# Four slots instead of five in each of the two rings of gathered expert rows

## The chip, the cores and the metric

The kernel runs on one core of one Trainium2 chip. The metric is the device time of one execution in microseconds (us), as the median of several runs. TensorE (PE), VectorE (DVE), ScalarE (ACT) and GpSimd (POOL) each have an instruction stream of their own; SyncE (SP) only issues DMAs here.

## The reference

One decoder layer over 1,024 positions of width 1,024, in float32. Its first half is attention: `h = x + W_out(concat[headnorm(A(xn)), subln(B(xn))])`, where A is a dilated sliding-window attention of 8 heads and B a differential attention of 4 heads with two softmax maps each. The second half is a retrieval over 16,384 single-neuron experts:

```python
def peer_layer(x, w_q, sub_keys, u_table, v_table):
    ...                     # scores of 8 heads against 2 x 128 sub-keys, top 16 of each, top 16 of the 256 sums
    u = u_table[ic]         # per token 128 rows of 1024 floats
    act = gelu(einsum('cd,chkd->chk', xc, u)) * gates
    v = v_table[ic]         # per token another 128 rows of 1024 floats
    return einsum('chk,chkd->cd', act, v)
```

The result is `h + peer_layer(RMSNorm(h))`. Every token picks its own 128 experts, so its u rows and v rows have to be gathered by index.

## The kernel before

The 1,024 tokens are 8 tiles of 128, one token to a partition. A first phase projects all tiles to q, k and v with the whole of w_in in SBUF. Then come stages e = 0 to 9. In stage e the *front* works on tile e: attention maps, output projection, norm, queries, and the selection of the 128 experts of each token. At the same time the *experts* of tile e-1 are worked off. A stage is written out by hand as 64 slots. Slot s of a stage holds two picks, 2s and 2s+1, of the 128 of the tile, and on every engine pieces of the front stand between them: in slots 0 to 19 the attention (lines 501, 517 and 530 on PE, line 839 on DVE, lines 695 and 704 on ACT), in slots 21 to 24 the output projection (line 545), in slots 27 to 50 the expert queries (line 566, whose weights SP loads through a ring of its own), in slots 32 to 55 the selection, and in slots 56 to 59 six operations of DVE of 2,048 elements each (lines 941, 945 and 949). Stage 0 has a front alone; from stage 1 on rows are gathered; stages 8 and 9 have no front.

For pick g, counted over all tiles:

- POOL issues the gather of the u row (`gather_u`, line 408): one row of 1,024 floats, 4 KB, for each of the 128 tokens, 512 KB in all, into slot g % RU of `u_ring`. Before it may issue, DVE must have finished with the row that stood in that slot (`u_used`).
- DVE multiplies that row with the normed token and sums it (`dot_row`, line 1026); the sum goes through Gelu on ACT in groups of 16, and times the gate it is the activation.
- POOL issues the gather of the v row (`gather_v`, line 417), again 512 KB, into slot g % RV of `v_ring`. It has to wait for PE's last use of that slot (`v_used`).
- ACT makes a diagonal matrix of the activations (`make_diag`, line 680), and PE multiplies it with the v row and adds it up in PSUM (`add_row`, line 590). The trace shows each addition as four passes.

POOL has one queue, in program order: u of pick g, then v of pick g - 24 (LAG = 24). A wait of a v gather therefore also holds up the next u gather. PE too takes `add_row` of pick 2s - 24 and 2s - 23 in slot s, between pieces of the front of the same slot, while DVE takes `dot_row` of picks 2s and 2s + 1 there. The first 24 gathers are of u alone, the last 24 of v alone.

The order of the gathers on POOL:

```python
for g in range(SEQ + LAG):
    if g < SEQ:
        gather_u(g)
    if g >= LAG:
        gather_v(g - LAG)
```

All SBUF of this part is carved out of one fixed buffer (`big`), so a slot fewer leaves room unused and moves what is carved behind it.

Of the kernel before, what the change touches and what calls it, by code (L numbers as in the profile page):

```python
# [36 lines left out]
LAG = 24  # L37
LAST_STAGE = TILES + 1
GROUPS = PICKS // TOPK
RU = RV = 5  # L40
RW = 4
RD = 4

# [50 lines left out]
def hybrid_layer(nc, x, attn_norm_g, w_in, q_norm_a, k_norm_a, out_norm_a, q_norm_b, k_norm_b,  # L94
# [4 lines left out]
    with ctx:  # L99
# [3 lines left out]
        def sem(name):  # L103
            return ctx.enter_context(nc.semaphore(name))

        def signal(name, per_tile, unit=1):
            return Signal(sem(name), per_tile, unit)
# [39 lines left out]
        def carve(cols):  # L147
            at[0] += cols
            assert at[0] <= BIG
            return big[:, at[0] - cols:at[0]]  # L150

        w_out_sb = carve(KC * D).rearrange("p (k n) -> p k n", k=KC)
        w_ring = carve(RW * 2 * COLS).rearrange("p (r k n) -> p r k n", r=RW, k=2)
        u_ring = carve(RU * D).rearrange("p (r n) -> p r n", r=RU)
        v_ring = carve(RV * D).rearrange("p (r n) -> p r n", r=RV)
# [56 lines left out]
        w_loaded = [signal(f"w_loaded{r}", 2 * PH // RW, 16) for r in range(RW)]  # L212
        u_loaded = [sem(f"u_loaded{r}") for r in range(RU)]
        v_loaded = [sem(f"v_loaded{r}") for r in range(RV)]
# [186 lines left out]
        def _(pool):  # L401
            def gather_u(g):
                t, p = divmod(g, PICKS)
                if p == 0:
                    pool.wait_ge(idx_ready.sem, idx_ready.at(t, 1))
                if g >= RU:
                    pool.wait_ge(u_used.sem, g - RU + 1)
                nc.gpsimd.indirect_dma_start(  # L408
                    out=u_ring[:, g % RU, :], out_offset=None, in_=peer_u,
                    in_offset=bass.IndirectOffsetOnAxis(ap=idx[:, t % 2, p:p + 1], axis=0))\  # L410
                    .then_inc(u_loaded[g % RU], 16)

# [682 lines left out]
```

## Time and profile before

| | |
|---|---|
| median of 3 runs | 3675.07 us (3672.83 to 3680.99) |
| the profiled execution's own time | 3687.51 us |
| its span | 3685.7 us |
| mean granted TensorE clock | 0.965 |
| gathers | 2 x 1024, 512 KB each |
| first gather is issued at | 567.54 us of the span |

The profile gives for each engine its busy time, the waits and what ended them, and the stretch of the span in which they lie. Line numbers are those of the kernel. "PE psum L590" is the instruction of line 590 on PE that writes psum. The idle time before an instruction is put down to whatever came last; "issue" means nothing that the profile shows, and a POOL instruction always has 0.30 us of it, also where the releaser named had come long before its slot was asked for.

### The profile page before, as it was taken

What the parts mean: (1) busy time and instruction counts of PE and PEld (TensorE: products, weight loads), DVE (VectorE), ACT (ScalarE), POOL (GpSimd) and SP (SyncE); (2) the same over time, 40 slices, a digit from 0 to 9 for tenths busy, and PEclk for the clock granted to TensorE, in tenths of its full rate; (3) what the DMA queues carried; (4) which work ended last, traced back from release to release, by engine and by line L of the source; (5) the groups of instructions that cost most, each with busy time, mean ns of one, the idle gap of its engine ahead of it and who ended that gap; (6) DMA issues with size and microseconds to landing.
All of it is one profiled execution on the core that took longest, in us unless ns stands there. A gap on an engine that the chain in (4) does not pass through costs nothing.

```text
span 3685.7 us, 29514 instructions
## 1 busy us (share of the span) xinstructions
PE 3044.6 (83%) x9440; PEld 1473.1 (40%) x9440; DVE 2061.8 (56%) x4508; ACT 762.7 (21%) x1695; POOL 2249.5 (61%) x2052
## 2 busy tenths in 40 slices
PE   7999665887988799878987898879887998766677
PEld 3444343442444244434443344435442544322223
DVE  1333257577556755675657565765577455754442
ACT  2111102211321132113211232123211321111111
POOL 0000006777777777777777777775777567777775
PEclk9999776999999999999999999999999999999999
DMA  5000237999999999999999999998999899999998
GB/s 175 23 23 17 106 103 282 384 406 370 373 378 406 373 359 378 406 384 356 356 404 406 345 345 385 406 365 311 377 405 376 279 327 403 381 356 368 365 365 307
DMA packets 351792, 1191.68 MB, mean 323 GB/s; under 512 B 41376, under 2 KB 41504, under 8 KB 351648
## 3 DMA queue, kind: packets, MB, share of 16 engines
q0 software_dynamic: 294912, 1073.87, 76.9%
q1 hardware_dynamic: 56736, 116.03, 8.6%
q8 instruction: 73, 1.20, 0.1%
q14 instruction: 71, 0.58, 0.0%
HBM read 1177.17 MB, written 12.58 MB: 323 GB/s over the span
## 4 chain that ended last, share of the span: by engine, by line
PE 42%; POOL 24%; DMA 20%; issue 9%; DVE 2%; another core or an unknown queue 2%; SPq 1%; ACT 1%; ACTq 0%; DVEq 0%
PE psum L590 21%; DMA big<-in_peer_v,big 18%; POOL big L408 12%; POOL big L417 11%; PE psum L446 8%; PE psum L501 3%; PE psum L566 3%; PE psum L530 2%; PE psum L545 2%; PE psum L517 1%; DMA big<-in_peer_u,big 1%; SPq L325 1%; DMA big<-in_x 0%; DMA big<-in_c_iota 0%
## 5 line engine op out<-in xcount | busy, mean ns | idle before, releaser
L590 PE MATMUL psum<-big 128*128 128x512 f32 x4096 | 2004.6, 618 | 478.6 <-DMA big<-in_peer_v,big 397.2
L1026 DVE CUSTOM_DVE_ANT_0 big<-big 128x1024 f32<-128x1024 f32 x1024 | 1247.3, 1225 | 854.7 <-DMA big<-in_peer_u,big 748.9
L408 POOL DMA_INDIRECT big<-in_peer_u,big x1024 | 1111.8, 1086 | 883.4 <-DVE big L953 567.1
L417 POOL DMA_INDIRECT big<-in_peer_v,big x1024 | 1137.4, 1111 | 540.9 <-PE psum L590 248.3
L590 PEld LDWEIGHTS psum<-big 128*128 128x128 f32 x4096 | 720.4, 192 | 1535.6 <-DMA big<-in_peer_v,big 803.5
L680 ACT ACTIVATE big<-ident,big 128x128 f32<-128x128 f32 x1024 | 394.9, 398 | 1878.9 <-PE psum L590 1357.9
L446 PE MATMUL psum<-big 128*128 128x512 f32 x768 | 339.4, 602 | 2.3 <-DMA big<-in_w_in 1.2
L566 PEld LDWEIGHTS psum<-big 128*128 128x128 f32 x2048 | 250.8, 195 | 61.7 <-issue 54.7
L839 DVE CUSTOM_DVE_ANT_0 big<-psum,big 128x128 f32<-128x128 f32 (+7 forms) x128 | 96.9, 757 | 308.7 <-PE psum L501 192.4
L566 PE MATMUL psum<-big 128*128 128x128 f32 x2048 | 253.2, 278 | 8.9 <-ACT big L729 5.6
L501 PE MATMUL psum<-KT,big 64*128 64x512 f32 (+3 forms) x384 | 170.2, 553 | 64.6 <-DVE big L839 46.0
L446 PEld LDWEIGHTS psum<-big 128*128 128x128 f32 x768 | 147.5, 194 | 183.9 <-issue 180.4
L530 PEld LDWEIGHTS psum<-V,big 128*128 128x128 f32 x864 | 117.8, 204 | 58.3 <-issue 39.8
L695 ACT ACTIVATE big<-big 128x128 f32<-128x128 f32 (+7 forms) x128 | 99.2, 775 | 184.3 <-DVE big L839 158.9
L530 PE MATMUL psum<-V,big 128*128 128x64 f32 (+1 forms) x864 | 121.1, 288 | 11.9 <-ACT big L704 8.7
L545 PE MATMUL psum<-big 128*128 128x512 f32 x256 | 121.7, 603 | 2.9 <-issue 1.6
L501 PEld LDWEIGHTS psum<-KT,big 64*128 64x128 f32 x384 | 67.9, 205 | 140.1 <-issue 80.0
L704 ACT ACTIVATE big<-psum 128x128 f32<-128x128 f32 (+7 forms) x96 | 62.1, 647 | 261.0 <-PE psum L517 180.0
L777 DVE TENSOR_TENSOR big<-big 128x2048 f32<-128x2048 f32 x8 | 18.3, 2292 | 153.8 <-ACT big L656 153.8
L1026 DVE DVE_READ_ACCUMULATOR2_ANT big<- 128x1 f32 x1024 | 83.8, 82 | 0.0
L545 PEld LDWEIGHTS psum<-big 128*128 128x128 f32 x256 | 49.4, 194 | 65.8 <-issue 63.1
L517 PEld LDWEIGHTS psum<-ident,big 128*128 128x128 f32 x432 | 56.5, 152 | 48.0 <-issue 40.5
(120 smaller groups left out, 1266.8 us busy)
## 6 DMA issues: line engine op xcount, KB each, us to landing
big<-in_w_peer_q SPq DMA_DIRECT2D x128, 512.0 KB
big<-in_peer_u,big POOLq DMA_INDIRECT x1024
big<-in_peer_v,big POOLq DMA_INDIRECT x1024
big<-in_w_in SPq DMA_DIRECT2D x6, 2048.0 KB, 17.8
big<-in_x SPq DMA_DIRECT2D x16, 512.0 KB, 3.7
q_scratch<-big SPq DMA_DIRECT2D x8, 512.0 KB, 2.8
big<-q_scratch SPq DMA_DIRECT2D x8, 512.0 KB
big<-in_w_out SPq DMA_DIRECT2D x1, 4096.0 KB, 15.1
```

Of the source, the lines that this page charges most:

```text
L408: nc.gpsimd.indirect_dma_start(out=u_ring[:, g % RU, :], out_offset=None, in_=peer_u, in_offset=bass.IndirectOffsetOnAxis(ap=idx[:, t % 2, ...
L417: nc.gpsimd.indirect_dma_start(out=v_ring[:, g % RV, :], out_offset=None, in_=peer_v, in_offset=bass.IndirectOffsetOnAxis(ap=idx[:, t % 2, ...
L446: last = nc.tensor.matmul(psum[:, n, :], xnT[:, k, :], w_in_sb[:, c, k, :], start=(k == 0), stop=(k == KC - 1))
L501: last = nc.tensor.matmul(pS_row[:, n:n + w], QT[half, pair, :], KT[half, pair, n:n + w], start=True, stop=True)
L530: last = nc.tensor.matmul(dst, turned[:, k, :], V[:, k, c0:c0 + w], start=(k == 0), stop=(k == t))
L545: last = nc.tensor.matmul(pS[:, n, :], turned[:, k, :], w_out_sb[:, k, n * COLS:(n + 1) * COLS], start=(k == 0), stop=(k == KC - 1))
L566: last = nc.tensor.matmul(pT[:, j % 2, i * P:(i + 1) * P], w_ring[:, n % RW, k, i * P:(i + 1) * P], turned[:, 2 * kp + k, :], start=(kp == ...
L590: last = nc.tensor.matmul(pAcc[:, n, :], diag[:, g % RD, :], v_ring[:, g % RV, n * COLS:(n + 1) * COLS], start=(p == 0), stop=(p == PICKS ...
L680: e.activation(diag[:, g % RD, :], ident[:, :], ACT.Copy, scale=act[:, t % 2, p:p + 1])\
L695: e.activation(row_, row_, ACT.Exp, bias=neg_max[:, m:m + 1], scale=-1.0, accum_out=den[:, m:m + 1]).then_inc(p_ready.sem, 1)
L839: v.tensor_tensor_reduce(out=S[:, buf, 0:w], in0=pS_row[:, 0:w], in1=mask[:, SEQ - w:SEQ], scale=-SCALE, scalar=-3.0 * NEG, op0=ALU.add, o ...
L1026: v.tensor_tensor_reduce(out=row_, in0=row_, in1=hn[:, t % 2, :], scale=1.0, scalar=0.0, op0=ALU.mult, op1=ALU.add, accum_out=dot[:, t % 2 ...
```

## The change

Each ring has four slots instead of five. The modulus of the slot numbers and the threshold of the waits follow from the two constants: the gather of pick g waits until the row of pick g - 4 has been used, not that of pick g - 5. Two of the semaphores of the rings (one of each) are gone with the slots. No operation is added or taken away on any engine.

```diff
@@ -37,7 +37,7 @@
 LAG = 24
 LAST_STAGE = TILES + 1
 GROUPS = PICKS // TOPK
-RU = RV = 5
+RU = RV = 4
 RW = 4
 RD = 4
```

## Rows read from the trace of the kernel before

**Rows 1.** The page's busy times, and what the DMA queues moved.
```profile
PE 3044.6 (83%) x9440; PEld 1473.1 (40%) x9440; DVE 2061.8 (56%) x4508; ACT 762.7 (21%) x1695; POOL 2249.5 (61%) x2052
...
q0 software_dynamic: 294912, 1073.87, 76.9%
q1 hardware_dynamic: 56736, 116.03, 8.6%
```

**Rows 2.** Groups by line, POOL: busy us, mean ns of one, idle before and its releasers.
```profile
L417 POOL DMA_INDIRECT big<-in_peer_v,big x1024 | 1137.4, 1111 | 540.9 <-PE psum L590 248.3 <-issue 237.8 <-remote 54.8
L408 POOL DMA_INDIRECT big<-in_peer_u,big x1024 | 1111.8, 1086 | 883.4 <-DVE big L953 567.1 <-issue 309.2 <-DVE big L1026 7.2
```

**Rows 3.** Windows: stretch, its us, busy PE, PEld, DVE, ACT, POOL, PEclk, DMA share, GB/s.
```profile
700.00:850.00 150.00, 125.38 (x488) 69.60 (x488) 98.25 (x271) 24.83 (x60) 107.84 (x101) 0.99 1.03 404
...
2490.00:2580.00 90.00, 87.58 (x332) 47.60 (x331) 51.12 (x92) 34.02 (x64) 48.16 (x50) 0.98 0.88 308
...
2870.00:2990.00 120.00, 112.31 (x427) 62.32 (x427) 59.40 (x104) 41.95 (x74) 57.36 (x60) 0.94 0.80 272
...
3050.00:3190.00 140.00, 120.84 (x477) 67.17 (x477) 93.76 (x262) 22.94 (x57) 103.90 (x95) 1.00 1.02 401
...
3260.00:3632.00 372.00, 260.69 (x517) 89.96 (x516) 161.04 (x267) 51.92 (x136) 273.26 (x258) 0.98 0.97 368
```

**Rows 4.** Chain of waits in the attention of tile 7.
```profile
2899.63 1.77 PE psum L590 x4
2901.40 0.87 PE psum L517 x8
2902.27 1.91 PE psum L501 x4
```

**Rows 5.** POOL's waits, 2870 to 2990 us: us in total, times, longest.
```profile
POOL big L417 <- PE psum L590: 45.9, 23, 4.3
```

**Rows 6.** POOL's waits, 1730 to 1800 us.
```profile
POOL big L417 <- PE psum L590: 8.5, 7, 4.3
```

**Rows 7.** Timeline of stage 8 (no front): start us, us, instruction, idle before.
```profile
3359.72 1.00 POOL L408 DMA_INDIRECT big<-in_peer_u,big  x1 [0.30 <-issue]
...
3361.02 0.94 POOL L417 DMA_INDIRECT big<-in_peer_v,big  x1 [0.31 <-issue]
...
3362.26 1.02 POOL L408 DMA_INDIRECT big<-in_peer_u,big  x1 [0.30 <-issue]
...
3366.37 1.22 DVE L1026 CUSTOM_DVE_ANT_0 big<-big 128x1024 f32<-128x1024 f32 x1 [1.32 <-DMA big<-in_peer_u,big]
...
3367.67 1.98 PE L590 MATMUL psum<-big 128*128 128x512 f32 x4 [0.59 <-issue]
```

**Rows 8.** Chain of waits, 1248 to 1261 us, the end of a 406 GB/s stretch.
```profile
1249.73 8.88 DMA big<-in_peer_v,big
1258.61 0.04 issue
1258.66 2.00 PE psum L590 x4
1260.66 0.09 issue
1260.74 1.99 POOL big L417
```

**Rows 9.** Timeline of the start, u gathers alone.
```profile
567.54 1.07 POOL L408 DMA_INDIRECT big<-in_peer_u,big  x1 [567.08 <-DVE big L953]
...
572.01 1.22 DVE L1026 CUSTOM_DVE_ANT_0 big<-big 128x1024 f32<-128x1024 f32 x1 [3.33 <-DMA big<-in_peer_u,big]
...
579.12 0.94 POOL L408 DMA_INDIRECT big<-in_peer_u,big  x1 [0.60 <-DVE big L1026]
580.65 0.94 POOL L408 DMA_INDIRECT big<-in_peer_u,big  x1 [0.60 <-DVE big L1026]
...
585.66 1.57 POOL L408 DMA_INDIRECT big<-in_peer_u,big  x1 [0.30 <-issue]
587.53 1.18 POOL L408 DMA_INDIRECT big<-in_peer_u,big  x1 [0.30 <-issue]
...
607.46 0.93 POOL L417 DMA_INDIRECT big<-in_peer_v,big  x1 [0.30 <-issue]
```

**Rows 10.** POOL's timeline at the end, v gathers alone.
```profile
3669.65 0.94 POOL L417 DMA_INDIRECT big<-in_peer_v,big  x1 [0.78 <-PE psum L590]
3671.36 0.94 POOL L417 DMA_INDIRECT big<-in_peer_v,big  x1 [0.78 <-PE psum L590]
```

## The prediction

> **What bounds the kernel now.** I read the page first: PE is busy 83% of the span, POOL 61%, and the gathers' queue carries 1073.87 of some 1190 MB [rows 1]. That names no bound, so I went to POOL's groups. A gather keeps POOL 1.111 us (v) or 1.086 us (u), and 0.30 us lie before each. One pick, a u and a v gather, therefore costs POOL 1.111 + 1.086 + 2 x 0.30 = 2.80 us when it never waits, and 1024 picks cost 2867 us. That is most of the 3118 us between the first gather at 567.5 us and the end of the span. Waits on the slots (PE L590 248.3 us, DVE L1026 7.2 us, each with 0.30 us of ordinary issue in it) are small beside that [rows 2]. The waits matter all the same where POOL's lead over its users is full, and so I cut the time from 567 us on into windows. They are of three kinds:
>
> - B, the stretch in slots 27 to 55 where the weights of the queries are loaded too: DMA share 1.02 to 1.03 and 401 to 406 GB/s, more than anywhere else. The DMA engines are the bound. There are seven such stretches, one to each front from tile 1 to 7; the first and the last stand in [rows 3].
> - A, the attention of the late tiles: PE is busy 87.58 of 90 us and 112.31 of 120 us, DMA falls to 308 and 272 GB/s [rows 3], and the chain there goes through PE alone [rows 4]. PE is the bound, the rings stand full, and POOL waits for PE before nearly every v gather: 23 times for 45.9 us in tile 7 [rows 5], still 7 times for 8.5 us in tile 4 [rows 6]. Such stretches are in the fronts of tiles 3 to 7, five in all.
> - C, the rest, stage 8 above all: 368 GB/s [rows 3], and POOL issues with nothing but 0.30 us before each gather [rows 7]. POOL is the bound.
>
> **The change, part by part.** No instruction is added. What changes is how far POOL may run ahead: four picks of u and four of v instead of five. So the question is in which stretches the fifth slot is used, and what is lost when it goes.
>
> *C, running evenly.* In [rows 7] the pick takes 3362.26 - 3359.72 = 2.54 us. The u gather issued at 3359.72 (the 931st) is consumed by the dot that starts at 3366.37 and takes 1.22: its slot is taken for 7.87 us. The v gather of 3361.02 (the 907th) is used by the addition at 3367.67 for 1.98: 8.63 us. With 0.30 to restart POOL, the loop of v is 8.93 us long, so 8.93/2.54 = 3.5 slots carry it. Four are enough, with 4 x 2.54 - 8.93 = 1.2 us to spare; five have 3.8 to spare. Cost 0 when it runs evenly. The cover is gone where the user of a row is over 1.2 us late; I come to that under the small fillings.
>
> *B.* Here a v gather's landing takes 8.88 us after its issue of about 0.94, and PE frees the slot 2.04 us later [rows 8]; with 0.09 to restart, the loop is 12.0 us. Over four slots that is 3.0 us a pick, against the 2.8 to 2.9 of POOL's pace. But in C the landing came within 3367.67 - 3361.96 = 5.7 us of the end of the issue [rows 7]: some 3 us of the 8.88 are queueing behind other transfers. If fewer gathers are in the queue the landing shortens, until 4 x 2.85 = 11.4 us are met. The DMA engines remain full, so inside B it costs nothing.
>
> *A.* PE sets the pace and the rows lie ready. One row fewer lies ready; PE does not see it. Cost 0 inside A.
>
> *The crossings out of A and B.* This is where the fifth slot pays. While A or B lasts, POOL is held to its users' pace plus the ring. When the stretch ends and POOL is the bound again, it starts from a lead of five picks now and of four afterwards. From then on POOL runs at its own 2.80 us a pick [rows 2], and nothing gives the missing pick back until the next crossing. So each crossing costs one pick, 2.80 us. Seven crossings out of B and five out of A make 12 x 2.80 = 33.6 us. For each the least is 0 (the lead is not full when the stretch ends, or the following stretch does not need it), and the most is 2.80.
>
> *The start.* 24 u gathers alone take 607.46 - 567.54 = 39.9 us, 1.66 each. Where they wait for DVE they come every 580.65 - 579.12 = 1.53 us, a loop of 5 x 1.53 = 7.7 us [rows 9]. With four slots the interval is at most 7.7/4 = 1.92, and at least that of an empty queue: the first row is used 4.47 us after its issue started, plus 1.22 for the dot and 0.60 before the next issue, 6.29/4 = 1.57. So 24 gathers cost between 0 and 24 x (1.92 - 1.66) = 6.2 us; I take the middle, 3 us.
>
> *The end.* 24 v gathers alone come every 1.71 us, PE's pace [rows 10]. An empty loop of v is 8.63 + 0.30 us at most [rows 7], 8.93/4 = 2.2 us; the first row's 4.47 us plus 1.98 and 0.78 give 7.23/4 = 1.8. The row is nearer to the latter: 24 x 0.1 = 2 us, at most 12. I count it among the small fillings.
>
> *Small fillings.* Between crossings DVE or PE is late by some us now and then (the six long DVE operations in slots 56 to 59, runs of front passes on PE), and the lead goes to between four and five picks. No row prices this. It costs at most one pick of 2.80 us in each of eight stages, 22 us, at least nothing; I take 9 us with the end's 2.
>
> A rule of the Trainium skill speaks against any loss. First the row: the first gather, with nothing before it, is used 4.47 us after its issue began [rows 9]. DMA: Bandwidth & Descriptors, section Anatomy of one DMA, gives some 2.0 us plus the bytes at 436 GB/s for a DMA from GpSimd, which for 512 KB makes an estimate of 3.2 us. By that a loop of v would be 3.2 + 1.98 + 0.3 = 5.5 us and three slots would do even when the queue is empty; the trace's loop is longer, and it is the fullness at the crossings that counts. By the page the change would cost nothing.
>
> **The sum.** 33.6 + 3 + 9 = 46 us. The profiled execution took 3687.5 us (span 3685.7 us), so it would take 3733 us; the median of the runs shown, 3675.1 us, stands 0.34% below that execution, and with the same sum it becomes 3721 us. I say 3720 us, 1.2% more. About 0.2%, 7 us, is what a measurement of this kernel can tell from no change.
>
> **The rivals.**
>
> *No change.* The crossings cost nothing: PE is the bound in A and the DMA engines in B, and after B a queue of landings is there that four slots also fill. For it: POOL waits for slots in some 8% of its time from the first gather on (255.5 of 3118 us, [rows 2]), and four slots carry the even loop. Against it: after B and A comes C, where POOL is the bound. Time: start and half the small fillings at most, 0 to 7 us, 3675 to 3682 us. Chance 12%.
>
> *Faster.* A gather that POOL issues right after DVE's dot takes 0.94 us, at 579.12 and 580.65 us [rows 9]; one that POOL issues when it likes takes 1.57 and 1.18 there. The long ones cost in all 2249.5 - 2048 x 0.94 = 324 us. If POOL and DVE hinder each other, a tighter ring ties POOL's issues to the end of its users' work and makes them shorter. It decides from the point where it saves more than the 46 us, a seventh of the 324: at a quarter, 81 us, the time is 3675 + 46 - 81 = 3640 us. Against it: in most of C POOL does not wait for slots even with four, and its issues stay where they are. Chance 6%. SBUF — State Buffer, section Who interferes with whom, in the Trainium skill has a rule of that kind: GpSimd and a VectorE operation in a two-port mode hold a shared port in turn, the other blocked for the whole instruction. That the long issues here are such waits no row proves.
>
> *Much slower.* The landing time in B does not shorten, because it is the weight loads that lie in front of the gathers and not other gathers. Then the pick takes 3.0 us there or more instead of 2.85. The seven stretches hold about 980 us, 340 picks; at 3.0 us that is 51 us more, at 3.3 us 150. On top of the 46: 3770 to 3870 us. Against it: the share of the weights is small, 116.03 MB in all against 1073.87 [rows 1]. Chance 10%.
>
> **How the numbers follow.** Crossings as summed 72%, no change 12%, faster 6%, much slower 10%. The forecast's own range: the five crossings out of A alone and nothing else give 14 us (3689); all 33.6 with 22 of small fillings, 6 at the start and 12 at the end give 74 us (3749). The range that holds eight in ten reaches down into the first rival, to 3680, and up to the lower end of the third, 3770. Slower by over 0.2% 0.83, within 0.2% 0.11, faster by over 0.2% 0.06.
>
> **What would show it.** After the change, in stage 8 the pick still takes about 2.5 to 2.9 us and POOL still issues with 0.30 us before it; the gathers take 1.1 us on average; waits of L417 on PE L590 rise from 248 us by some 40 to 100, in B and A, not in C. In B the chain's DMA pieces are below 8 us, and the stretches still show over 400 GB/s. It would be wrong if B falls clearly below 400 GB/s (much slower), if POOL's busy time falls by tens of us (faster), or if each stage lasts as long as now although POOL waits more.

## The result, and the profile after

The kernel with four slots takes 3716.8 us (median of 4, 3712.3 to 3722.2) against 3675.2 us; the ratio is 1.0116, 95% interval 1.0097 to 1.0134. It is slower by 41.5 us, 1.2%; 3720 us was forecast. The profiled execution has a span of 3717.9 us, 32.2 us more than that of before. The differences read from the two traces add up to these 32 us, not to 41.5: the profiled execution of before took 12 us more than the median of its kernel, that of after 3 us more.

The order and the number of the instructions are the same. POOL's groups by line (busy us, mean ns of one, idle before it and its releasers), the answer to [rows 2]:

```profile
L417 POOL DMA_INDIRECT big<-in_peer_v,big x1024 | 1156.4, 1129 | 554.2 <-PE psum L590 300.1 <-issue 232.7 <-remote 21.3
L408 POOL DMA_INDIRECT big<-in_peer_u,big x1024 | 1106.0, 1080 | 890.4 <-DVE big L953 568.9 <-issue 307.0 <-DVE big L1026 14.5
```

The whole loss can be read from POOL, because it is never out of work between the first gather and the last. Busy time went from 2249.2 to 2262.4 us, +13.2. Idle time before the gathers went from 540.9 + 883.4 to 554.2 + 890.4, +20.3, of which 1.8 us are the later first gather. Within the idle time something was exchanged: waits for PE rose by 51.8 us (248.3 to 300.1) and for DVE by 7.3, while "remote" fell by 33.5 (54.8 to 21.3). I come to that at the end.

The windows that answer to those of [rows 3], moved to where the same work now lies (columns as there):

```profile
705.00:855.00 150.00, 124.27 (x488) 68.38 (x486) 95.08 (x259) 23.96 (x58) 109.57 (x100) 1.00 1.03 402
2525.00:2615.00 90.00, 87.07 (x330) 47.18 (x329) 50.65 (x93) 33.56 (x65) 47.96 (x51) 0.98 0.89 305
2905.00:3025.00 120.00, 117.44 (x463) 64.76 (x461) 62.20 (x110) 43.23 (x78) 62.23 (x64) 0.97 0.83 283
3085.00:3225.00 140.00, 118.32 (x459) 64.70 (x457) 92.33 (x261) 23.25 (x56) 101.50 (x93) 1.00 1.01 394
3294.00:3664.00 370.00, 264.43 (x519) 91.36 (x520) 160.89 (x268) 53.81 (x138) 275.11 (x259) 0.97 0.98 370
```

Little moves. The attention of tile 7 (third line) is even denser on PE than it was, 117.4 of 120 us against 112.3. Stage 8 (last line) carries 370 GB/s where it carried 368. The stretches with the weight loads (first and fourth) are still nearly full. The table that helps is one of stages. Its numbers are differences of the start times of the first u gather of each tile in POOL's timeline, in us; the last column runs to the end of the span:

```
                        stage 1   2      3      4      5      6      7    8 to the end
before                  346.1  380.9  383.3  385.0  390.0  396.2  411.6   425.1
four slots              355.5  386.7  384.5  385.4  399.7  403.1  410.5   423.2
difference               +9.4   +5.8   +1.2   +0.4   +9.7   +6.9   -1.1    -1.9
four slots again        352.5  383.8  386.7  388.7  399.0  405.6  408.5   421.6
```

The last row is a second execution of the same kernel, u4v4 of the experiments. The two executions with four slots differ by 0.7 to 3.3 us in each stage, so a difference of 1 or 2 us in one stage means nothing.

The first and the last of the start times of after that it is made of, and the first v gather:

```profile
569.34 1.07 POOL L408 DMA_INDIRECT big<-in_peer_u,big  x1 [568.88 <-DVE big L953]
...
614.32 1.40 POOL L417 DMA_INDIRECT big<-in_peer_v,big  x1 [0.30 <-issue]
...
3294.69 0.94 POOL L408 DMA_INDIRECT big<-in_peer_u,big  x1 [0.30 <-issue]
```

The start, 24 u gathers alone, now takes 614.32 - 569.34 = 45.0 us, 5.1 more; that is half of what stage 1 loses. Stage 8, which has no front, loses nothing: where the work is even, four slots carry it, as the prediction said. All else is lost beside a front, but not once for each crossing: stages 3, 4 and 7, which have both crossings of the prediction, lose 0.5 us together (4.0 us by the second execution), where six crossings of 2.80 us were to make 16.8.

### The profile page after: what moved, and what is told of

It is laid out like the page before. It is cut to its first block, busy times and chain, and to the rows that moved or that the text cites. A ratio compares the mean times of both kernels' runs of the same rounds, so it can differ in the third digit from the quotient of the medians.

```text
span 3717.9 us, 29514 instructions
## 1 busy us (share of the span) xinstructions
PE 3051.0 (82%) x9440; PEld 1468.0 (39%) x9440; DVE 2066.1 (56%) x4508; ACT 767.6 (21%) x1695; POOL 2262.6 (61%) x2052
## 4 chain that ended last, share of the span: by engine, by line
PE 42%; DMA 24%; POOL 20%; issue 8%; DVE 3%; SPq 1%; ACT 1%; another core or an unknown queue 0%; ACTq 0%; DVEq 0%
DMA big<-in_peer_v,big 22%; PE psum L590 21%; POOL big L408 10%; POOL big L417 10%; PE psum L446 8%; PE psum L501 3%; PE psum L545 3%; PE psum L566 3%; PE psum L530 2%; DMA big<-in_peer_u,big 1%; PE psum L517 1%; SPq L325 1%; DMA big<-in_x 0%; DMA big<-in_c_iota 0%
## 5 line engine op out<-in xcount | busy, mean ns | idle before, releaser
L408 POOL DMA_INDIRECT big<-in_peer_u,big x1024 | 1106.0, 1080 | 890.4 <-DVE big L953 568.9
L417 POOL DMA_INDIRECT big<-in_peer_v,big x1024 | 1156.4, 1129 | 554.2 <-PE psum L590 300.1
```

Of the source, the lines that this page charges most:

```text
L408: nc.gpsimd.indirect_dma_start(out=u_ring[:, g % RU, :], out_offset=None, in_=peer_u, in_offset=bass.IndirectOffsetOnAxis(ap=idx[:, t % 2, ...
L417: nc.gpsimd.indirect_dma_start(out=v_ring[:, g % RV, :], out_offset=None, in_=peer_v, in_offset=bass.IndirectOffsetOnAxis(ap=idx[:, t % 2, ...
```

## The experiments

Each group was timed beside the kernel before on one chip. The groups differ: the kernel before takes 3613 us in groups 1 and 3, 3676 in group 2 (3675 beside the change itself) and 3693 in group 4. So only ratios, or differences within one group, are compared.

**Which ring? Group 1, kernel before 3613.4 us.** The edits:

```diff
-RU = RV = 5
+RU, RV = 5, 4     # u5v4
+RU, RV = 4, 5     # u4v5
+RU, RV = 4, 6     # u4v6
+RU, RV = 3, 3     # u3v3
```

> Only the ring of v rows has four slots, the ring of u rows keeps five. Theory (crossings, v decides): in the trace of the kernel before POOL waits 248 us in all for PE before a v gather and 7 us for DVE before a u gather, so it is the v ring whose fullness limits POOL's lead, and nearly all of the loss of the change must be here: +35 to +42 us against the kernel before. Rival 1 (what counts is the number of transfers that can be under way, 9 instead of 10): half the loss, about +20 us. Rival 2 (u decides): 0 to +5 us.

> Only the ring of u rows has four slots, the ring of v rows keeps five. Theory (crossings, v decides): only the start with its 24 u gathers alone is touched, some 5 us, and elsewhere u fills seldom: +3 to +8 us against the kernel before. Rival 1 (number of transfers under way): about +20 us. Rival 2 (u decides): +35 to +42 us.

> Four slots for u, six for v: as many slots in all as before. Theory (v decides): v may run a pick further ahead, the crossings gain what four slots lost, perhaps somewhat less, as a lead of six is reached less often; minus the start's 5 us: -10 to -30 us against the kernel before. Rival 1 (number of transfers under way, ten as before): within 5 us of the kernel before. Rival 2 (u decides): +35 us or more.

> Three slots in each ring. Theory: the loop of a v slot in even running is 8.93 us, over three slots 2.98 us a pick, which is above POOL's own pace of 2.80 to 2.9; so besides a second pick at each crossing (another +35 us) all of the stretches where POOL had been the bound become bound by the ring, 600 picks and more by 0.1 to 0.4 us: +130 to +280 us against the kernel before, and POOL waits before most v gathers. Rival (each slot has the same price wherever it is taken from): twice the change's loss, +80 to +90 us.

Measured: u5v4 3670.1 us, ratio 1.0149 (1.0132 to 1.0165); u4v5 3656.0, 1.0115 (1.0093 to 1.0137); u4v6 3652.3, 1.0109 (1.0092 to 1.0126); u3v3 3897.6, 1.0785 (1.0763 to 1.0808).

The theory that the v ring alone decides falls: u4v5 was to cost 3 to 8 us and costs 42.6, u4v6 was to gain and loses 38.9. Rival 1, the number of transfers under way, falls with it, since u4v6 has ten slots like the kernel before. POOL's waits show what happens. First u5v4, then u4v5 (us in total, times, longest):

```profile
POOL big L417 <- PE psum L590: 337.6, 434, 6.0
...
POOL big L408 <- DVE big L1026: 1.2, 2, 0.6
```

```profile
POOL big L408 <- DVE big L1026: 200.3, 161, 3.5
POOL big L417 <- PE psum L590: 104.6, 274, 1.5
```

The wait moves to whichever ring is the shorter, and the loss is of the same kind, 1.49% and 1.15%. That the trace of before showed POOL waiting for PE 248 us and for DVE 7 us did not mean that the u ring had room to spare. I read it so: of two rings in step the v ring closed a little sooner. Since POOL issues u and v in turn from one queue, its lead is that of the shorter ring, and slots in the longer one are idle (the sixth v slot of u4v6 brought 3.7 us against u4v5, with intervals that overlap). u4v6 also rules out that the loss comes from what a shorter ring moves in `big`: its ten slots leave everything behind the rings where it was, and it loses 1.09% all the same.

With three slots POOL waits more than with four all over. The whole trace, and then stage 8 alone (3448 to 3811 us):

```profile
POOL big L417 <- PE psum L590: 582.8, 647, 5.7
...
POOL big L408 <- DVE big L1026: 56.3, 53, 2.8
```

```profile
POOL big L417 <- PE psum L590: 51.7, 111, 2.9
```

The size, 284 us, is just above what I expected (130 to 280). As to its place, it has to be read beside a kernel of the same group. Stage 8 in u3v3, and then in u5v4 (columns as in [rows 3]):

```profile
3448.00:3811.00 363.00, 255.53 (x509) 87.53 (x508) 158.49 (x263) 53.24 (x136) 264.12 (x254) 0.99 0.98 371
```

```profile
3278.00:3604.00 326.00, 249.53 (x503) 85.62 (x502) 157.04 (x261) 52.80 (x135) 247.19 (x254) 0.99 1.03 409
```

From its first gather to the end of the span stage 8 takes 435.3 us with three slots, against 388.3 in u5v4: 47 us more, the most of any stage. There is no front there. A pick takes 2.86 us instead of 2.58. Of the 127 v gathers in the window 111 are put down to PE's last use of their slot, with 51.7 us of waits (in u5v4 94, 30.1 us), and a v gather keeps POOL 1.11 us instead of 1.00. That is the even loop that was expected to bind, a little shorter than reckoned (3 x 2.86 = 8.6 us against 8.93). Beside the fronts stage 1 takes 34 us more than in u5v4, stages 2 to 4 take 27 to 30 more each, stages 5 to 7 take 20, 17 and 11 more. So three slots cost in both places, in even running and beside a front. The loss grows faster than the slots go: 1.2 to 1.5% for the fifth, some 6.5% more for the fourth.

**The change beside them, and the other direction. Group 2, kernel before 3676.3 us.**

```diff
-RU = RV = 5
-RW = 4
+RU = RV = 4              # u4v4, RW stays 4
+RU = RV = 5; RW = 2      # u5v5w2
+RU = RV = 6; RW = 2      # u6v6w2
```

> The change itself (four slots each), beside the experiments. One ring alone cut to four cost 1.49% (v) and 1.15% (u) on a chip where the kernel before takes 3613 us, and with u cut to four two more slots for v gave nothing back. Theory now (the smaller ring gates POOL's lead, since u and v go through one queue in turn): both at four is hardly worse than the worse of the two, +1.2 to +1.8%. Rival (each ring has its own price and they add): +2.6%.

> The ring of query weights has two slots instead of four, the row rings five as before. It is the control for the next one. Weights are used four loads to every six slots of the stage, so SP is late more often: between 0 and +15 us against the kernel before if the queries wait now and then, -5 us if fewer weights under way leave the gathers more room.

> Six slots in each row ring, paid for with two slots of the ring of weights. Theory (the smaller ring gates, and each stretch in which the lead is full loses a pick per slot missing): the sixth slot is worth less than the fifth (46 us by the sum, 42 measured), as a lead of six is reached less often, some 15 to 30 us less than with five slots and two weight slots. Rival (five are enough, the bound is elsewhere): within 5 us of it.

Measured: u4v4 3722.1 us, 1.0129 (1.0098 to 1.0160); u5v5w2 3693.9, 1.0045 (1.0027 to 1.0064); u6v6w2 3692.3, 1.0048 (1.0030 to 1.0067).

The prices of the rings do not add: both together cost 1.29%, not 2.64%. This agrees with the shorter ring setting the lead. The sixth slot is worth nothing here, against 15 to 30 us expected. So five is where the cushion ends, at least with two slots of weights; six with four do not fit, because `big` has 152 columns left of 34,560 and two rows need 2,048. None of the ring sizes is faster than the kernel before.

**Which stretches? Group 3, kernel before 3613.9 us.** Two kernels take away one kind of crossing each, and each was run with five slots and with four. In w5 and w4 the queries of tiles 1 to 7 are computed from weights of which seven eighths are stale; in a5 and a4 the attention sees 128 keys only.

```diff
+                dst, src = w_ring[:, n % RW], w_peer_q[...]...       # w5, w4
+                if t:
+                    dst, src = dst[:, 0, 0:P], src[:, 0, 0:P]
+                sp.dma_start(dst, src).then_inc(w_loaded[n % RW].sem, 16)
...
         def reach(t):                                               # a5, a4
-            return (t + 1) * P
+            return P
...
-                for k in range(t + 1):
+                for k in range(1):
```

> Five slots each, but from tile 1 on the loads of the query weights are cut to 512 bytes a partition instead of 4 KB (the queries of tiles 1 to 7 are then wrong; the instructions of all engines stay). It takes the stretches B away: 59 MB less, some 145 us of DMA time at 406 GB/s, of which only what is bound there comes back. POOL's pace of 2.80 us and its stalls remain, so 60 to 150 us less than the kernel before. It is the base of w4.

> The same with four slots each. Theory of the prediction (a pick of 2.80 us for each crossing out of A and out of B): without B five crossings, the start and the small fillings remain, so 19 to 27 us more than w5. Rival 1 (it is B alone: the windows of the two traces put 27 of the 32 us between pick 32 and pick 112 of the stages): 0 to 10 us more than w5. Rival 2 (the fifth slot is a cushion against lateness everywhere, not only at crossings): 35 us or more above w5.

> Five slots each, but the attention takes the first 128 keys alone for every tile (the output of the attention is then wrong; masks, exponentials, transposes and products of the other keys are left out). It takes the stretches A away, in which PE is the bound: stages 5 to 7 last 387 to 409 us from first gather to first gather and stage 2 to 4 some 381; without A all should last about 375: 60 to 90 us less than the kernel before. It is the base of a4.

> The same with four slots each. Theory of the prediction: seven crossings out of B, the start and the small fillings remain, 42 - 14 = 28 us more than a5 (24 to 33). Rival 1 (B alone): the full 38 to 45 us. Rival 2 (a cushion everywhere): 35 us or more, so like rival 1; the two are told apart by w4.

Measured: w5 3586.6 us, 0.9935 (0.9913 to 0.9957); w4 3627.8, 1.0040 (1.0025 to 1.0054); a5 3507.7, 0.9717 (0.9699 to 0.9734); a4 3572.9, 0.9888 (0.9870 to 0.9905). The fifth slot is worth 41.2 us without the stretches B and 65.2 us without the stretches A. Both bases gave back less or more than expected (27 us for w5, where 60 to 150 were; 106 us for a5, where 60 to 90 were). w5 moves 51.4 MB less, not the 59 that I had reckoned.

What the edits do to the stretches stands in two windows (columns as in [rows 3]): the stretch B of stage 1 in w5, and the attention of stage 7 in a5.

```profile
767.00:856.00 89.00, 77.17 (x277) 39.50 (x276) 69.15 (x201) 14.26 (x36) 69.48 (x65) 1.00 1.01 385
```

```profile
2759.00:2864.00 105.00, 86.38 (x223) 37.07 (x221) 56.41 (x127) 30.11 (x92) 80.27 (x81) 1.00 1.02 405
```

In w5 the stretches B are gone (385 GB/s where before has 407, and no wait for a slot from pick 64 of a stage on, with five slots or four). In a5 PE is no longer the bound in the attention, but DMA now is (405 GB/s where before has 291). So w5 and w4 are the cleaner pair; a5 and a4 have turned the stretches A into something like B.

This speaks against the prediction's sum and against rival 1 (B alone), which both wanted less than 28 us from w4. It agrees with rival 2, a cushion against lateness and not only at crossings. The stages, as above:

```
                        stage 1   2      3      4      5      6      7    8 to the end
w5 to w4                 +8.2   +5.4   +4.4   +6.0   +1.0  +10.9   +6.0    +4.3
a5 to a4                +17.4   +9.7   +9.0   -1.4   +5.8   +4.2  +11.1   +10.0
```

POOL's waits in w5, then in w4 (the lines lie three lower, 411 for 408, 593 for 590 and so on):

```profile
POOL big L420 <- PE psum L593: 184.6, 246, 5.6
POOL big L411 <- DVE big L1029: 1.6, 2, 1.0
```

```profile
POOL big L420 <- PE psum L593: 247.5, 343, 5.7
...
POOL big L411 <- DVE big L1029: 13.9, 15, 1.7
```

75 us of waits more, and a span of 45 us more. Without A the loss grows instead of shrinking. In A PE is the bound and does not care when POOL is late, as long as it still finds its rows ready. With A gone nothing absorbs it. I argue that from the stages (7 loses nothing in the full kernel and 11.1 us in a4) and have not shown it by itself; that the attention of a4 has become a stretch in which DMA is the bound, where a shorter lead may cost too, is the other reading.

**A third kind of stretch? Group 4, kernel before 3693.3 us.** The trace of after shows POOL held by its slots at a place that I had not counted: the output projection, where PE alternates four passes of front and four of addition. Timeline, POOL and then PE:

```profile
1459.09 0.94 POOL L417 DMA_INDIRECT big<-in_peer_v,big  x1 [0.67 <-issue]
1460.33 0.93 POOL L408 DMA_INDIRECT big<-in_peer_u,big  x1 [0.30 <-issue]
1462.52 0.94 POOL L417 DMA_INDIRECT big<-in_peer_v,big  x1 [1.26 <-issue]
...
1465.95 0.94 POOL L417 DMA_INDIRECT big<-in_peer_v,big  x1 [1.02 <-PE psum L590]
...
1469.39 1.21 POOL L417 DMA_INDIRECT big<-in_peer_v,big  x1 [1.26 <-PE psum L590]
```

```profile
1462.08 1.88 PE L545 MATMUL psum<-big 128*128 128x512 f32 x4
1463.80 1.88 PE L590 MATMUL psum<-big 128*128 128x512 f32 x4
1465.52 1.88 PE L545 MATMUL psum<-big 128*128 128x512 f32 x4
1467.23 7.03 PE L590 MATMUL psum<-big 128*128 128x512 f32 x16
1476.31 2.71 PE L590 MATMUL psum<-big 128*128 128x512 f32 x4 [2.05 <-DMA big<-in_peer_v,big]
```

An addition every 3.43 us instead of every 2.8: POOL waits 0.7 to 1.3 us before each v gather. At 1467.23 PE does four additions at once and then stands still 2.05 us for a v row. The same stretch of before (1440 to 1465 us there) has POOL issuing with 0.30 us before all but one of its gathers; that one waits 2.52 us. In the 50 us about this place POOL idles as long before its v gathers in both traces (8.7 us before, 10.2 us after), so what is seen here is how the wait comes about and not what it costs. It is a stretch that every tile has. The edit holds the lead at four there alone:

```diff
+            def lead(at, most):
+                return 4 if 44 <= at % PICKS < 76 else most
...
-                    pool.wait_ge(u_used.sem, g - RU + 1)
+                    pool.wait_ge(u_used.sem, g - lead(g, RU) + 1)
...
-                    pool.wait_ge(v_used.sem, g - RV + 1)
+                    pool.wait_ge(v_used.sem, g - lead(g + LAG, RV) + 1)
```

> Five slots, but POOL holds its lead to four picks where its position in the stage is between pick 44 and pick 75 (two stricter thresholds, nothing else). That is the output projection, the norm and the first queries of every tile (slots 22 to 37), a stretch that neither crossing of the prediction is in: A ends before it, B ends after it. Theory now (the fifth slot is used in a third kind of stretch, where PE is held up by the output projection and the norm, and then again at the start of the queries): in the trace with four slots 37 of 60 us of the waits for slots that came new in the stages with a front lie in picks 48 to 79, so +15 to +30 us against the kernel before. Theory of the prediction (only the ends of A and B count): 0 to +5 us. Rival (a cushion everywhere, in proportion to the picks held, a quarter): about +10 us.

Measured: 3707.6 us against 3693.3, ratio 1.0035 (1.0017 to 1.0054): some 13 us, 6 to 20. That is more than the 0 to 5 us that the prediction's list of crossings allows. It is a third of the change's 42 us, from a quarter of the picks. It does not tell the other two apart: 10 us and the lower end of 15 to 30 both lie in 6 to 20.

One thing could spoil the test. When POOL is at pick 44 its users leave slot 19, the last one of the attention. A pick of lead that was gained in A would be lost here too, and five of 2.80 us are 14 us. The trace speaks against it. In stages 3 to 7 POOL issues pick 44 with only two rows still ahead of its users, with and without the edit, and it never waits for a slot at picks 44 to 47. Of the 27.5 us of waits for slots (beyond 0.30 us each) at picks 48 to 75 of the stages with a front, which before does not have, 12.7 lie in stages 1 and 2, where there is no stretch A.

## Why the prediction was right in its number and not in its sum

- *POOL, PE and DMA are the bounds by turns, and no instruction changes.* Held. POOL's busy time is 1.10 us a gather on average as before, and the windows have the same three kinds.
- *Even running costs nothing.* Held: stage 8 took 423.2 us after and 425.1 before. In group 3, where stage 8 runs at 2.57 to 2.60 us a pick, it and the end took 4.3 us (w5 to w4) and 10.0 us (a5 to a4) more with four slots. The working took the fastest pace, 2.54 us a pick; the average of stage 8 in the traces of before and after is 2.87 and 2.86 us (364.6 and 363.3 us from the first to the last u gather). The loop of 8.93 us bore a second forecast: three slots were to be bound by it, and in u3v3 they are, at 2.86 us a pick where its group has 2.58.
- *The start, 0 to 6 us, taken as 3.* 5.1 us in the profile. *The end, 2 us.* Nothing: 60.5 us from the last u gather to the end of the span before, 59.9 after.
- *Twelve crossings of 2.80 us, 33.6 us.* This is the step that failed. That a pick of lead is lost at the end of a stretch in which POOL was held, and costs 2.80 us there, was not tested by itself. But the list of the places, ends of A and B alone, was wrong. Taking seven of the twelve away (w5, w4) left 41.2 us where 19 to 27 were to remain, and taking the other five away (a5, a4) left 65.2 us where 24 to 33 were. A stretch that was in no crossing costs 13 us where the lead is held short (cap44_76). Of the seven stages with a front, three with both crossings lose 0.5 us together. The waits on slots rose as foretold (L417 on PE by 51.8 us), but not in A: beyond 0.30 us each they went from 89 to 99 us at picks 0 to 47 of stages 1 to 7, where the attention is, and from 10 to 65 us at picks 48 to 127. The total of 33.6 us came near by luck: too much for the ends of A and B, too little for the many short fillings.
- *Small fillings, 9 us, at most 22.* Mis-sized. By what the pairs left, they and not the crossings carry most of the loss. The rows that should have told me are those of the even loop [rows 7]. Four slots leave 1.2 us to spare at the fastest pace and 4 x 2.86 - 8.93 = 2.5 at the average one of stage 8; five leave 3.8 and 5.4; three leave nothing (3 x 2.86 - 8.93 = -0.35). The fronts are full of pieces of 1.7 to 2.3 us on PE and DVE, about as long as the spare of four slots and shorter than that of five. That would make three slots dear everywhere, four moderately so beside a front, and the sixth useless, as measured. It is an explanation that fits all runs; none of them varied the length of a piece to test it.
- *No change* was refuted by the measurement. *Faster* too: POOL's gathers did not get shorter, they cost 13 us more in all. *Much slower* through landings in B that do not shorten did not come. The one DMA piece of the chain at the end of a stretch B is 8.63 us instead of 8.88 [rows 8], where I had said below 8, but one piece says little. Over all v gathers issued at picks 80 to 111 of stages 1 to 7 the mean from the start of the issue to the end of the addition went from 12.8 to 10.7 us, while a pick took 2.96 us before and 2.97 after. So the landings shorten by 2 us and B is all but free, as the working had it; two stretches carry 402 and 394 GB/s instead of 404 and 401.

```profile
1249.82 8.63 DMA big<-in_peer_v,big
```

Where in a stage the loss falls depends on whose clock one reads. Below are the differences between five slots and four, in us, summed over stages 1 to 7: first on POOL (start of the u gather of picks 0, 44, 76 and of the next tile's first), then on DVE (end of the dots of the same picks).

```
                              picks 0 to 43   44 to 75   76 to 127
POOL, before to after             +4.5         +22.9        +4.9
POOL, w5 to w4                   +13.9         +22.7        +5.3
POOL, before to cap44_76          +6.1         +14.6        +0.1
DVE, before to after              +2.6         +10.8       +18.2
DVE, before to cap44_76           +4.0          +3.3       +13.0
```

POOL loses most of it in the quarter that holds the output projection, the norm and the first queries, with stretches B and without. From before to after it loses no more in the attention than the start costs. Its users feel it later, most of it from pick 76 on. One of these rows compares two groups (cap44_76), and all are of one execution each; the two executions with four slots differ by up to 7 us in one of POOL's columns. What stays open is how much each kind of work in that quarter contributes, and why stages 3 and 4 lose so little.

## What to carry to other kernels

When one queue fills two rings in turn, the shorter ring sets the lead of both, and the wait table names only the one that closes first: cut or lengthen them together, and don't take a ring that nobody waits for as one with room to spare. Size a ring by the spare that is left over its even loop, slots times pace minus loop. Below zero the ring binds even running, as three slots did. Above it, compare the spare with the longest piece of other work that its users do between two rows; that second half is the explanation argued above, not a tested rule. Two tests tell a cushion from a bound: take away the stretch that is supposed to need the slot, with both sizes of ring, and hold the lead short in one stretch alone. Look whether the stretch is really gone or has only changed its bound, and compare stages only within one group of runs: read against a trace of another group, the 47 us that three slots cost in stage 8 look like 10.

## What the runs showed of the hardware

The same kernel takes 3613 us in groups 1 and 3, 3676 in group 2 and 3693 in group 4. That this is the chip is not shown: groups 1 and 2 have the same chip number on record, 13, with 3613 and 3676 us.

Some 30 to 40 us of the difference lie in stage 8, where there is no front. With four or five slots it takes 383 to 393 us in the traces of groups 1 and 3, at 2.57 to 2.60 us a pick (409 GB/s, DMA share 1.03 in the window of u5v4 above). In before, in after and in groups 2 and 4 it takes 415 to 425 us, at 2.82 to 2.87 us a pick (370 GB/s, 0.98 in after).

Another part is visible in POOL's pauses. In the trace of before POOL stands still 78 times, for 0.1 to 3.3 us beyond the usual 0.30 and 122 us in all, ahead of v gathers whose slot has been free for a while. I counted as free what began more than 0.6 us after the end of the last use of its slot. 28 of these are put down to "remote", 54.8 us. In group 3 w5 has 4 such pauses (3.5 us) and a5 9 (9.0 us), and no trace of groups 1 and 3 has a line "remote". In group 4, cap44_76:

```profile
POOL big L420 <- remote: 60.2, 36, 3.6
```

What these pauses are, no run shows. In the change they fell to 56 times and 70 us, while waits for slots rose from 112 to 183 us. The two overlap: a pause can cost nothing where POOL would have waited for a slot anyway. So where there are pauses a shorter ring may look cheaper than where there are none. The ratios for the shorter v ring (1.0149, without pauses) and for both rings (1.0116 and 1.0129, with them) go that way; their intervals overlap or touch, and that for the shorter u ring (1.0115, without) does not go that way. It is not shown.
